# Key and value columns of a second input projection computed as two pairs of chunks by the seven-product scheme

## The reference

```python
hn = _rmsnorm(h, attn_norm_w[l])
proj = hn @ w_in[l]
a_q, a_k, a_v, a_g, b_cq, b_ckv, b_kr, b_g = jnp.split(proj, list(splits), axis=-1)
```

## Time and profile before

| | us |
|---|---|
| median of 3 runs (1656.9 to 1657.13) | 1657.11 |
| the profiled execution | 1656.58 |
| its span | 1654.8 |
| TensorE busy in it | 1639.2 (99%) |
| granted TensorE clock | 0.999 |

### The profile page before, as it was taken

The page is one execution under the profiler, slowest core; times in us unless marked ns, Lnnn a source line. Parts: engine busy times, 40 slices in busy tenths (PEclk is TensorE's granted clock), DMA queues, the critical chain, the costliest instruction groups (busy, mean ns, idle before and its releaser), DMA issues.

```text
span 1654.8 us, 22346 instructions
## 1 busy us (share of the span) xinstructions
PE 1639.2 (99%) x8439; PEld 1361.3 (82%) x8439; DVE 708.9 (43%) x1764; ACT 782.2 (47%) x1699; POOL 708.8 (43%) x569
## 2 busy tenths in 40 slices
...
GB/s 232 116 119 61 124 82 127 77 52 115 175 181 192 128 222 251 153 155 77 164 197 199 173 175 213 218 83 136 68 158 65 141 52 77 102 102 123 244 244 102
DMA packets 118375, 234.82 MB, mean 142 GB/s; under 512 B 8475, under 2 KB 16220, under 8 KB 118124
## 3 DMA queue, kind: packets, MB, share of 16 engines
...
## 4 chain that ended last, share of the span: by engine, by line
PE 92%; DVE 3%; ACT 2%; issue 2%; POOL 1%; POOLq 0%; ACTq 0%; DVEq 0%
PE acc L617 21%; PE acc L619 20%; PE acc L618 20%; PE turn L714 3%; PE turn L982 2%; PE turn L639 2%; PE turn L702 1%; PE acc L758 1%; PE acc L757 1%; PE acc L759 1%; PE sc L630 1%; PE sc L631 1%; PE sc L931 1%; PE sc L956 1%; PE sc L689 1%
## 5 line engine op out<-in xcount | busy, mean ns | idle before, releaser
L1603 POOL TENSOR_TENSOR w_lo<-w_raw,w_hi 128x512 fp32r<-128x512 f32 x405 | 586.3, 1453 | 860.9 <-ACT w_hi L1098 850.3
L1098 ACT ACTIVATE w_hi<-w_raw 128x512 fp32r<-128x512 f32 x517 | 323.2, 628 | 496.5 <-PE acc L619 404.9
L617 PE MATMUL acc<-w_hi,setA_hi 128*128 128x512 f32 (+1 forms) x1344 | 544.1, 405 | 2.4 <-DVE setA_lo L1788 0.8
L619 PE MATMUL acc<-w_hi,setA_lo 128*128 128x512 f32 (+1 forms) x1344 | 521.1, 388 | 0.0
L618 PE MATMUL acc<-w_lo,setA_hi 128*128 128x512 f32 (+1 forms) x1344 | 519.4, 386 | 0.0
L617 PEld LDWEIGHTS acc<-w_hi,setA_hi 128*128 128x128 f32 x1344 | 252.8, 188 | 52.6 <-issue 6.9
L619 PEld LDWEIGHTS acc<-w_hi,setA_lo 128*128 128x128 f32 x1344 | 252.2, 188 | 53.2
L618 PEld LDWEIGHTS acc<-w_lo,setA_hi 128*128 128x128 f32 x1344 | 253.4, 189 | 40.0
L1956 DVE TENSOR_TENSOR w_lo<-w_raw,w_hi 128x512 fp32r<-128x512 f32 x112 | 78.7, 708 | 64.0 <-ACT w_hi L1098 63.9
L2060 DVE TENSOR_TENSOR sum_m<-sc,tmp_m 16x512 f32<-16x512 f32 (+1 forms) x9 | 5.9, 656 | 230.0 <-ACT tmp_m L1118 230.0
L1174 ACT ACTIVATE p_w<-sm,negm 128x256 f32<-128x256 f32 (+1 forms) x128 | 60.6, 474 | 57.1 <-DVE sink_d L1858 57.1
...
## 6 DMA issues: line engine op xcount, KB each, us to landing
w_raw<-in_w_in SPq DMA_DIRECT2D x48, 1024.0 KB, 5.2
w_raw<-in_swa_w_in SPq DMA_DIRECT2D x35, 1024.0 KB, 7.5
...
sum_out<-in_swa_w_out POOLq DMA_DIRECT2D x24, 512.0 KB, 7.5
sum_out<-in_w_out POOLq DMA_DIRECT2D x24, 512.0 KB, 7.8
sum_out<-sum_out POOLq DMA_DIRECT2D x16, 512.0 KB, 7.0
w_raw<-in_swa_w_out SPq DMA_DIRECT2D x8, 1024.0 KB, 5.4
...
```

What stands on the lines that cost most here:

```text
L617: mm(acc[t][:, 0:cols], hi[:, kc, rows], wh, start=(k == 0), stop=False)
L619: last = mm(acc[t][:, 0:cols], lo[:, kc, rows], wh, start=False, stop=(k == K - 1))
L1098: nc.scalar.activation(w_at(f)[0], raw_of(f), ACT.Copy).then_inc(done, 1)
L1603: nc.gpsimd.tensor_tensor(lo, raw_of(f), hi.bitcast(F32), ALU.subtract).then_inc(s_lo, 1)
```

## The change

Chunks 15 to 18 become two pairs, `k` (columns 1024 to 2047) and `v` (2048 to 3071), in `project_mid`. The order within a pair differs from `out1`: 24 tiles in three products, 24 in three, and 8 in the seventh. The meta rows are computed from the weight tiles and the weight sums of five of those products (`meta_product`), with a signed meta operand in `metaT`, for both chunks of the pair at once in the bank `acc[2]`. DVE forms the activation sums of the second block's input in four steps (`x1_sums`) during chunks 13 and 14, and the split of these sums (`split_s`, `split_s_lo`) is spread there too. The four rounds of weight sums for `k` go into chunks 1, 2, 5 and 9, those for `v` into chunks 12, 13, 14 and pair `k`, and those for `out2` move from chunks 15 to 18 into the low-rank chunks and the attentions. Each round now waits for the one before it. Transposes of the latent parts and of the rope key move to the end of pair `v` and into chunks 19 and 20, and ACT scales the combined blocks from SBUF (`scale_part`) where it scaled on evacuation.

```diff
+H2 = {"out1": [4, 5, 6, 7, 0, 1, 2, 3], "k": [8, 9, 10, 11, 12, 13, 14, 15], "v": [8, 9, 10, 11, 12, 13, 14, 15],
...
+SUM_AT = {"out1": 0, "x": 2, "out2": 6}
+SUM_SLOT = {}
+for slot, of in enumerate((("k", 0), ("k", 1), ("out1", 0), ("k", 2), ("out1", 1), ("out1", 2), ("out1", 3), ("k", 3),
+                           *(("v", i) for i in range(4)), *(("out2", i) for i in range(4)))):
+    SUM_SLOT[of] = slot
...
+                def sums_there(m):
+
+                    if m % 2 == 0:
+                        sp.wait_ge(s_sum2, 32 * (SUM_SLOT[c, m // 2] + 1))
+                        sp.wait_ge(s_sum4, 16 * (SUM_SLOT[c, m // 2] + 1))
...
+                if c in ("k", "v"):
+                    for m in range(8):
+                        load_tile(3 * m, w_a[H1[c][m]])
+                        sums_there(m)
+                        load_tile(3 * m + 1, sum_d[c][m, :, 1])
+                        load_tile(3 * m + 2, sum_d[c][m, :, 0])
+                    for m in range(8):
+                        load_tile(24 + 3 * m, w_a[H2[c][m]])
+                        load_tile(24 + 3 * m + 1, sum_d[c][m, :, 3])
+                        load_tile(24 + 3 * m + 2, w_b[H2[c][m]])
+                    for m in range(8):
+                        load_tile(48 + m, sum_d[c][m, :, 2])
...
             load_chunk(w_in2, 4608)
             load_chunk(w_in2, 4096)
-            for i in range(4):
-                load_chunk(w_in2, i * CW + 1024)
+            load_pair("k", a["w_in"])
+            load_pair("v", a["w_in"])
...
-                        pe.wait_ge(s_evac, 4 * E[14] + 8)
-                    turn4(50 + k - 5, (k - 5) % 2, [stage[:, t, (k - 5) * P:(k - 4) * P] for t in range(NT)])
-            for i in range(3):
-                for k in range(KC):
-                    for t in range(NT):
-                        if t == NT - 1:
-                            project_meta(i + 2, k, metaT)
-                        project(i + 16, k, t, setA_hi, setA_lo)
-            pe.wait_ge(s_turn_lo, 54 + EARLY)
...
+            def meta_product(c, p, unit, start, stop):
+
+                wh, wl = w_at(B[c] + p)
+                mm(acc[2][0:FULL, :], meta_window(unit), wh, start=start, stop=False)
+                last = mm(acc[2][0:FULL, :], meta_window(unit), wl, start=False, stop=stop)
+                if stop:
+                    last.then_inc(s_meta, 1)
...
+            def project_mid(c):
+
+                n, h1, h2, (X0, X1) = NTH[c], H1[c], H2[c], banks_of[c]
+                for m in range(8):
+                    for j in range(3):
+                        p = 3 * m + j
+                        wait_low(pe, B[c] + p)
+                        for i in range(2):
+                            top = slice(i * P, (i + 1) * P)
...
+                                product(c, p, i, setA_hi[:, h1[m], top], setA_lo[:, h1[m], top], X0[i], m == 0, m == 7)
+                                if i == 0:
...
+                                    meta_product(c, p, SIGNED_AT + 4 * h1[m], m == 0, False)
+                            elif j == 1:
...
+                                product(c, p, i, mx_hi[:, 0, m, top], mx_lo[:, 0, m, top], acc[i][:], m == 0, m == 7)
+                                if i == 0:
+                                    meta_product(c, p, 4 * h1[m], False, False)
+                            else:
...
+                                product(c, p, i, mx_hi[:, 1, m, top], mx_lo[:, 1, m, top], X1[i], m == 0, m == 7)
+                for m in range(8):
...
+                                product(c, p, i, setA_hi[:, h2[m], top], setA_lo[:, h2[m], top], X0[i], m == 0, m == 7)
+                                if i == 0:
+                                    meta_product(c, p, 4 * h2[m] + 1, False, False)
+                            elif j == 1:
...
+                                product(c, p, i, my_hi[:, 0, m, top], my_lo[:, 0, m, top], X1[i], m == 0, m == 7)
+                            else:
...
+                                product(c, p, i, my_hi[:, 1, m, top], my_lo[:, 1, m, top], acc[i][:], m == 0, m == 7)
+                                if i == 0:
+                                    meta_product(c, p, 4 * h2[m], False, m == 7)
+                for m in range(8):
+                    p = 48 + m
...
+                        turn4(48 + f, f % 2, [stage[:, t, f * P:(f + 1) * P] for t in range(NT)])
...
+                        product(c, p, i, setA_hi[:, h2[m], low], setA_lo[:, h2[m], low], X0[i], m == 0, m == 7)
+
+            project_mid("k")
+            project_mid("v")
...
+                    if c == 0:
+                        pe.wait_ge(s_turn_lo, 48 + k + 1 + EARLY)
                     for t in range(NT):
                         project(19 + c, k, t, cqT_hi, cqT_lo, K=4)
+                    if c == 0 and 1 <= k < 3:
+                        turn4(52 + k - 1, k - 1, [work[:, t, (k - 1) * P:k * P] for t in range(NT)])
...
+                    if k == 0 and slot:
+                        pool.wait_ge(s_sum4, 16 * slot)
+                    pool.dma_start(d[rows, :, k], (low_b, top_a, low_a, top_b)[k]).then_inc(s_block, 16)
...
-                    pool.wait_ge(s_block[c], 64 * (i + 1))
-                    pool.dma_start(d[rows, :, 1], top[:, :, 2], accum_op=ALU.add).then_inc(s_sum2[c], 16)
+                    pool.wait_ge(s_block, 64 * (slot + 1))
+                    pool.dma_start(d[rows, :, 1], top_b, accum_op=ALU.add).then_inc(s_sum2, 16)
...
                 elif k == 11:
-                    pool.wait_ge(s_sum2[c], 32 * (i + 1))
-                    pool.dma_start(d[rows, :, 0], d[rows, :, 1], accum_op=ALU.add).then_inc(s_sum3[c], 16)
+                    pool.wait_ge(s_sum2, 32 * (slot + 1))
+                    pool.dma_start(d[rows, :, 0], d[rows, :, 1], accum_op=ALU.add).then_inc(s_sum3, 16)
                 elif k == 14:
-                    pool.wait_ge(s_sum3[c], 16 * (i + 1))
-                    pool.dma_start(d[rows, :, 2], d[rows, :, 0], accum_op=ALU.add).then_inc(s_sum4[c], 16)
+                    pool.wait_ge(s_sum3, 16 * (slot + 1))
+                    pool.dma_start(d[rows, :, 2], d[rows, :, 0], accum_op=ALU.add).then_inc(s_sum4, 16)
...
                 split_lo(9, k)
+                block_sums("k", 3, k)
...
             for k in range(KC):
                 split_lo(12, k)
+                block_sums("v", 0, k)
...
+            for c in (13, 14):
                 for k in range(KC):
                     split_lo(c, k)
-                    if c == 13 and k == 12:
+                    block_sums("v", c - 12, k)
+                    if c == 13 and k == 13:
                         root(r_2[:], ss_1[:], NT, ROOT_2)
...
-                    if c == 15 and k == 3:
-                        root(r_cq[:], ss_cq[:], NT, ROOT_CQ)
-                    if c == 15:
-                        block_sums("out2", 0, k)
-            for i in range(3):
-                for k in range(KC):
-                    split_lo(16 + i, k)
-                    block_sums("out2", i + 1, k)
+            root(r_kv[:], ss_kv[:], NT + 1, ROOT_KV)
+            for k in range(KC):
+                pool.wait_ge(s_used, B["k"] + 3 * k + 4)
+                block_sums("v", 3, k)
+            root(r_cq[:], ss_cq[:], NT, ROOT_CQ)
+            for f in range(B[19], B[19] + AHEAD):
...
+                        if A.mla or i == 0:
+                            block_sums("out2", 1 + i if A.mla else 3, Q // 4)
...
                 split_lo(19, k)
+                block_sums("out2", 0, k)
...
 
-                n, pairs, sf = 4 * NTH[c] + 2 * b, slice(4 * b, 4 * b + 4), sums_of[c]
+                n, size, sf = 2 * (SUM_AT[c] + b), 2 if c == "x" else 4, sums_of[c]
...
+            def x1_sums(b):
+
+                sf = sums_of["x"]
+                for whole, first in ((whole_a, 2 * b), (whole_b, 8 + 2 * b)):
+                    last = V.tensor_tensor(whole[:], setA_hi[:, first:first + 2].bitcast(F32), setA_lo[:, first:first + 2].bitcast(F32), ALU.add)
+                after(dve, last)
+                (a1, a2), (b1, b2) = ((whole[:, :, 0:HALF], whole[:, :, HALF:S]) for whole in (whole_a, whole_b))
+                V.tensor_tensor(sf[:, 2], a2, a1, ALU.subtract)
+                after(dve, V.tensor_tensor(sf[:, 0], a2, b2, ALU.subtract))
+                after(dve, V.tensor_tensor(sf[:, 1], a1, sf[:, 0], ALU.subtract))
+                V.tensor_tensor(sf[:, 3], b1, sf[:, 1], ALU.subtract).then_inc(s_sf, 1)
...
+            def begin_mid(c):
+
+                n, (c_p, c_d, c_w, c_22), (X0, X1) = 2 * NTH[c], parts_of[c], banks_of[c]
+                group_lo(c, 24)
+                group_lo(c, 25)
+                for i in range(2):
+                    product_done(c, 3, i, 23)
+                    dve.wait_ge(s_p1, n + i + 1)
+                    V.tensor_tensor(c_d[:, i], X1[i], c_p[:, i], ALU.subtract).then_inc(s_v, 1)
+                group_lo(c, 26)
+                for i in range(2):
+                    dve.wait_ge(s_v, n + i + 1)
```

(11 more changed lines are left out.)

531 lines of the change are left out of this document (369 added, 162 removed).

## The result

| | before | changed |
|---|---|---|
| median, us | 1656.9 (9 runs) | 1660.99 (9 runs, 1656.69 to 1663.58) |
| the profiled execution, us | 1656.58 | 1661.9 |
| its span, us | 1654.8 | 1660.1 |

The ratio of the changed kernel to the one before is 1.0022, with a 95% interval of 1.0012 to 1.0032: about 4 us slower. The forecast was 1639.1 us, with a range of 1635.2 to 1645.0.

What follows compares the result with a forecast made beforehand. TensorE was taken as the bound, busy 99% of the span, time being matmul count times spacing. 1656.6 - 21.8 + 3.3 + 0.5 = 1638.6, and 0.5 more for the median: 1639.1 us, range 1635.2 to 1645.0.

Steps and rivals of the forecast that it cites:

- What is removed on TensorE, -21.8 us: Chunks 15 to 18 as pairs: 96 matmuls fewer at 0.2266 us each, -21.8 us, called the ceiling.
- In sum 2.0 us: Chunk 13 into 14: POOL held for landings makes low parts late; TensorE waits 0.7, 0.2 and 1.1 us.
- +3.3 with its addition: Chunks 13 and 14: POOL's 2.0 us, up to 4.5 with DVE's activation sums slowing low parts; middle +3.3, bounds 0 and 4.5.
- Queued behind these waits are only low parts; ACT's high parts and the loads follow TensorE: Chunks 13 and 14: step in POOL's chain claiming that its waits delay nothing but low parts.
- the loads, costed at nothing: Chunk 13: 8.2 us for a load, 8.7 beside sums; 0.5 late, covered by 3.9 to spare; nothing.
- DVE has the time: Activation sums on DVE: DVE, busy less than half the span, has room for them.
- Nothing: Pairs: free banks for the first product, chunk 14's evacuation ending about with it; no cost, up to 1 us.
- In a chunk of 12 matmuls ... that hides: Weight sums on POOL at 2.7 us per tile: POOL may be several microseconds late before TensorE notices.
- Low-rank chunks: One round of sums there, stores allowed 10.2 us to land; with pairs and the rest +0.5 us, bounds 0 and 6.
- the rival of late stores: Low-rank chunks: stores take 13.0 us, 2.8 over the allowance, and evacuations wait 2.8 + 2.5; 1644.4 us, chance 0.10.
- the last additions are spread over 40 us: Low-rank chunks: the argument against stores landing late beside this round of sums.

Runs made afterwards that it cites:

- E5: Changed kernel, but in the three rounds of weight sums in chunks 12 to 14 POOL waits for no landing, with as many bytes moved; 1655.76 us.
- E1: Changed kernel without the eight rounds of weight sums of k and v, their tiles loaded from the plain weights; 1649.36 us.
- E2: Changed kernel, but DVE does not form the activation sums of the second block, while splits and waits stay; 1655.29 us.
- E3: Changed kernel without the four rounds of weight sums of out2, its tiles loaded from the plain weights; 1653.48 us.
- E6: Changed kernel with rounds of weight sums moved: two in each of chunks 2 to 5, none in 1, 12 to 14 or 19 to 29; 1666.62 us.
- E7: E6, with ACT in chunk 19 issuing the small meta stores two steps sooner and the store of left after the evacuation; 1662.59 us.
- E11: Changed kernel with E7's shorter ACT list and rounds moved: one in chunk 1, four in chunks 2 to 5, none in pair out1 or chunk 30; 1639.70 us.
- E9: E6, but the eight rounds in chunks 2 to 5 use additions independent of one another, with as many transfers and bytes; 1652.71 us.

## Why the prediction was wrong

**What is removed on TensorE, -21.8 us: right.** The pairs took 22.4 us less in every kernel in which pair `k` started undisturbed. Part of the other 0.6 is the spacing: chunks 15 to 18 took 205.9 us for their 896 matmuls, 0.230 each and not 0.2266, which makes 22.1 for 96.

**"In sum 2.0 us", the chain of POOL in chunk 13, +3.3 with its addition: the mechanism was right, the term mis-sized.** It stands for 8.7 us, of which E5 gives 6.1 to the waits for landings and the clock behind them. The expectations count 9.4 us there; by the first matmul of pair `k` it is 8.7. The landings were as assumed: 10.4 us from the second addition (727.36 to 737.79) where I took 10.6, then 8.4 for 7.7 and 6.5 for 6.8; only the wait for the copies at step 7, 3.1 us, was missing. The step that failed is "Queued behind these waits are only low parts; ACT's high parts and the loads follow TensorE". Three things come from a held POOL or from its transfers that this sentence shut out:
- the loads, costed at nothing with 8.7 us against 8.2. They took 9.3 at the median, and ACT waited 3.3 and 6.0 us for two of them. In E1 it is 5.0. And they don't follow TensorE alone: each is issued when POOL has made a low part, so a held POOL issues them late;
- DVE. "DVE has the time" asked what DVE does to POOL and never what POOL's backlog does to DVE. A sum went from 0.69 to 4.64 us, ACT's splits stand in its order behind the sums, and high parts behind the splits, up to the first tile of pair `k`: a wait of 2.8 us where the working said "Nothing". It is 1.9 us in E5, 0.8 in E1 and absent in E2, which shows that without the sums chunk 14 loses nothing;
- the clock, 0.50 behind each of the long waits. No term had it.

**"In a chunk of 12 matmuls ... that hides": wrong.** The step asked only whether the low part is in time. `k` 0 cost 1.2 us in chunk 1, where ACT waited 9.2 us for a load (4.1 in the kernel before), and `out2` 1 to 3 cost 3.2 us in chunks 26 to 28 (E3). E6 shows why in the open: in an attention a DVE instruction on two columns is on TensorE's path, and POOL's low parts, once late, fall upon it.

**"Low-rank chunks", +0.5 with the pairs: off by the largest amount, +11.5.** A round there is worth about 5 us (E3: 6.8 less 1.7 of the clock), since stores of a megabyte land after 14 us for 5. That was the rival of late stores, 5.3 us with a chance of 0.10, and 13.0 us was its landing. Its argument against, that the last additions are spread over 40 us, failed. ACT's list, three stores issued ahead of the first evacuation of chunk 19, costs another 2.2 us, and 3.8 when the clock falls behind it (E6 to E7). It stood in the diff and had no term. In E11 2.7 us remain in chunks 19 to 25; 1.4 of them are the moved transposes themselves, which chunk 14 is rid of.

**The range.** By the medians the losses make 25.9 us (4.1 and the 21.8 gained) where the terms had 3.8. The cases were set up as rivals of which one at most would come, but they have one source, more transfers at the same time, and came together.

The scatter is in large part the clock's. 12 executions of E9 lie 11.0 us apart and 12 of E2 9.6, 20 of the kernel before 2.1. In E9 the mean granted clock goes from 0.999 in the fastest to 0.994 in the slowest, and 0.001 of 1650 us is 1.65 us, so that this is worth about 8 of the 11 us. In E2 it is 0.996 and 0.994, and about 3 of 9.6 us. Left open: the other 2 us of E9's 5.1 in chunks 2 to 5, the rest of the scatter in E2, and what decides whether the clock falls behind a pause.
